# Weight sums moved out of the down projections, and another order of the last projection's products

## The reference, cut to what matters

```python
x = first_block(x, ...)     # pooled mixer, then conv_ffn: up 1024 -> 2 x 2816, conv, gelu gate, down
for i in range(2):          # second_block
    m = fox_mixer(h) if i == 0 else s5_mixer(h)      # 16-head attention with forget gates; state space
    x = x + rmsnorm(m)
    x = x + rmsnorm((silu(h @ w_gate) * (h @ w_up)) @ w_down)     # up2/dn2, then up3/dn3
```

## Time and profile before

| | us |
|---|---|
| runs | 1713.88, 1724.02, 1733.31 |
| median | 1724.02 |
| the profiled execution's own time | 1720.28 |
| its span, first to last instruction | 1718.2 |
| PE busy | 1629.2 (95%) |
| DVE busy | 1102.5 (64%) |
| ACT busy | 724.7 (42%) |
| POOL busy | 319.5 (19%) |

### The profile page before, as it was taken

One profiled execution on the slowest core, in us unless ns is written; L12 is line 12 of the kernel. 1 busy time (PEld: TensorE's weight loads), 2 busy tenths in 40 slices (PEclk: granted clock), 3 DMA queues, 4 the chain that ended last, 5 costly groups with the idle time before them and its releaser, 6 DMA issues.

```text
span 1718.2 us, 23609 instructions
## 1 busy us (share of the span) xinstructions
PE 1629.2 (95%) x9069; PEld 1379.5 (80%) x9069; DVE 1102.5 (64%) x1774; ACT 724.7 (42%) x1158; POOL 319.5 (19%) x833
## 2 busy tenths in 40 slices
PE   6499999998999999999999999996999999999997
PEld 5378888886877877778888888785888889999786
DVE  6988666665664677756333337564756687777776
ACT  4454433322344767744222222233224444444564
POOL 2011401001307777720111111111011000000000
PEclk8789999999999999999999999998999999999999
DMA  8922257877542222225678878889994235555664
GB/s 354 374 74 99 98 197 193 215 204 214 153 120 83 68 72 71 81 80 172 232 193 182 181 223 208 224 238 247 248 244 122 92 116 183 182 183 184 181 189 145
DMA packets 176961, 297.20 MB, mean 173 GB/s; under 512 B 31713, under 2 KB 115025, under 8 KB 173522
## 3 DMA queue, kind: packets, MB, share of 16 engines
q1 hardware_dynamic: 141842, 225.44, 39.8%
q0 software_dynamic: 20096, 62.92, 16.6%
q10 hardware_dynamic: 14912, 7.34, 1.7%
HBM read 277.84 MB, written 80.73 MB: 209 GB/s over the span
## 4 chain that ended last, share of the span: by engine, by line
PE 74%; DVE 11%; DMA 8%; ACT 3%; issue 2%; SPq 0%; POOL 0%; ACTq 0%; DVEq 0%
PE bank L2194 23%; PE bank L2196 22%; PE bank L2195 22%; DMA raw<-in_dn 3%; DMA u_scratch<-us 2%; DVE ada L1426 2%; DVE w_lo L1323 1%; PE bank L2557 1%; DMA cc<-in_s_c 1%; PE bank L2530 1%; DVE prod L1673 1%; DVE r_tab L1675 1%; DVE r_tab L1672 1%; ACT w_hi L853 1%; PE bank L2686 1%
## 5 line engine op out<-in xcount | busy, mean ns | idle before, releaser
L2194 PE MATMUL bank<-hh,w_hi 128*128 128x512 f32 (+1 forms) x1440 | 521.1, 362 | 7.3 <-DVE w_lo L1323 3.4
L2195 PE MATMUL bank<-hl,w_hi 128*128 128x512 f32 (+1 forms) x1440 | 517.4, 359 | 0.0
L2196 PE MATMUL bank<-hh,w_lo 128*128 128x512 f32 (+1 forms) x1440 | 517.0, 359 | 0.0
L1323 DVE TENSOR_TENSOR w_lo<-raw,w_hi 128x1024 fp32r<-128x1024 f32 x320 | 373.5, 1179 | 210.8 <-ACT w_hi L853 205.7
L853 ACT ACTIVATE w_hi<-raw 128x1024 fp32r<-128x1024 f32 x320 | 325.3, 1021 | 415.4 <-DMA raw<-in_dn 175.4
L2194 PEld LDWEIGHTS bank<-hh,w_hi 128*128 128x128 f32 x1440 | 274.2, 190 | 48.9 <-DVE w_lo L1323 3.8
L2196 PEld LDWEIGHTS bank<-hh,w_lo 128*128 128x128 f32 x1440 | 274.3, 190 | 39.9
L2195 PEld LDWEIGHTS bank<-hl,w_hi 128*128 128x128 f32 x1440 | 274.5, 191 | 39.0
L2194 PE MATMUL bank<-w_hi,hid 128*128 128x512 f32 x352 | 138.6, 394 | 0.9 <-ACT kt L1014 0.9
L2195 PE MATMUL bank<-w_lo,hid 128*128 128x512 f32 x352 | 137.1, 389 | 0.0
L2196 PE MATMUL bank<-w_hi,hid 128*128 128x512 f32 x352 | 137.1, 389 | 0.0
(11 more groups left out here) (352 smaller groups left out, 2570.6 us busy)
## 6 DMA issues: line engine op xcount, KB each, us to landing
raw<-in_up SPq DMA_DIRECT2D x94, 512.0 KB, 3.8
raw<-in_dn SPq DMA_DIRECT2D x55, 512.0 KB, 5.8
ada<-in_ada_w SPq DMA_DIRECT2D x24, 1024.0 KB, 8.3
v_v_scratch<-in_up POOLq DMA_DIRECT2D x30, 768.0 KB, 7.8
v_scratch<-in_dn POOLq DMA_DIRECT2D x24, 704.0 KB, 6.3
raw<-in_fox_in SPq DMA_DIRECT2D x32, 512.0 KB, 3.5
raw<-in_up SPq DMA_DIRECT2D x57, 256.0 KB, 2.9
raw<-in_s_w SPq DMA_DIRECT2D x24, 512.0 KB, 5.3
```

The source lines that it names most:

```text
L1323: dve.tensor_tensor(w_lo[:, n % RING, 0:w], raw[:, n % RING, 0:w], w_hi[:, n % RING, 0:w].bitcast(F32), ALU.subtract).then_inc(lo_done, 1)
L2194: pe.matmul(dst, w_h, r_h, start=first, stop=False, skip_group_check=True)
L2195: pe.matmul(dst, w_h, r_l, start=False, stop=False, skip_group_check=True)
L2196: return pe.matmul(dst, w_l, r_h, start=False, stop=last, skip_group_check=True)
```

## The change

It does two things. First, the order on POOL: the 56 up sums now come first and the 32 weight sums last. Of the up sums 24 wait for the slots 20 to 43 (counts 21 to 44, in up1), 8 for the value slots 68 to 75, and 24 lie between the turn tables: one after each table, a second one after each odd table. These last ones wait only for each other. The weight sums wait for the slots from 110 on (counts from 111, in up2). SP's two waits on `sum_step` are changed to fit. Second, the products of the last down projection run as P1 P5 P6 P7 P4 P3 P2, with the operands, banks, sources and the additions between them permuted; s4 is formed at place 1 and s3 at place 2.

```diff
-        A_RAW = [a11_s1[:, :, 0, :], s2[:, :, :], s3[:, :, :], a11_s1[:, :, 1, :], a12_a22[:, :, 1, :], s4[:, :, :],
+        A_RAW = [a11_s1[:, :, 0, :], a11_s1[:, :, 1, :], s2[:, :, :], s3[:, :, :], a12_a22[:, :, 1, :], s4[:, :, :],
...
-        PROD_BANK = (BX, BY, BW, BZ, BY, BZ, BX)
+        PROD_BANK = (BX, BZ, BY, BW, BY, BZ, BX)
...
-            sp.wait_ge(sum_step, 16 * (DOWN_SUMS + 8 * len(SUM_CHUNKS)))
+            sp.wait_ge(sum_step, 16 * UP_SUMS)
...
-            sources = (q3[0], v_dram[1], v_dram[2], v_dram[0], v_dram[3], q3[3], q3[2])
-            sp.wait_ge(sum_step, 16 * DOWN_SUMS)
+            sources = (q3[0], v_dram[0], v_dram[1], v_dram[2], v_dram[3], q3[3], q3[2])
+            sp.wait_ge(sum_step, 16 * (UP_SUMS + 32))
...
-                    if i in (2, 5):
-                        act.wait_ge(comb_done, 4 + c + 1)
+                    if i == 3:
+                        act.wait_ge(comb_done, 4 + len(A_CHUNKS) + c + 1)
...
                     if i == 1:
+                        own.add(dve.tensor_tensor(s4[:, k0:k1, :], a12_a22[:, k0:k1, 0, :], s2[:, k0:k1, :], ALU.add))
+                    if i == 2:
                         own.add(dve.scalar_tensor_tensor(s3[:, k0:k1, :], s2[:, k0:k1, :], -1.0, a12_a22[:, k0:k1, 1, :],
                                                          ALU.mult, ALU.subtract))
-                        own.add(dve.tensor_tensor(s4[:, k0:k1, :], a12_a22[:, k0:k1, 0, :], s2[:, k0:k1, :], ALU.add))
+                    if i in (1, 2):
...
-                        if s == 0 and i == 2:
+                    if s == 0 and i == 3:
+                        for j in range(2):
                             dve.wait_ge(p1_done, PAIRED + j + 1)
                             dve.tensor_tensor(u2[:, j, :], bank[BY[j]][:, :], p1[:, j, :], ALU.add).then_inc(y_step, 1)
-                        if s == 0 and i == 3:
+                    if s == 0 and i == 4:
+                        for j in range(2):
                             dve.wait_ge(y_step, Y_STEPS + j + 1)
                             dve.tensor_tensor(u3[:, j, :], bank[BW[j]][:, :], u2[:, j, :], ALU.add).then_inc(y_step, 1)
...
             for t, ((to, src, add), (j0, j1)) in enumerate(itertools.product(steps, SUM_CHUNKS)):
-                    pool.wait_ge(slot_mm, start + t + 1)
-                    pool.wait_ge(sum_step, 16 * (DOWN_SUMS + t))
+                    if t:
+                        pool.wait_ge(sum_step, 16 * t)
...
+                    yield
+
+            sums = up_sums()
+            for t in range(24):
+                pool.wait_ge(slot_mm, S_UP1 + 19 + t)
+                next(sums)
+            for t in range(KT):
+                pool.wait_ge(slot_mm, S_V + 1 + t)
+                next(sums)
             for k in range(PAIRS // 2):
                 turn_tables(k)
-            up_sums(S_UP2 + 2)
+                next(sums)
+                if k % 2:
+                    next(sums)
+            assert next(sums, None) is None
+            weight_sums(S_UP2 + 2)
...
-                    if i == 2:
+                    if i == 1:
                         pe.wait_ge(val_done, 2 * HT)
```

More of the change, by code:

```diff
@@ L85 @@
 Y_STEPS = 4 * PAIRED
-DOWN_SUMS = 32
 SUM_CHUNKS = ((2, 5), (5, 8), (8, 11), (12, 15), (15, 18), (18, 20), (20, 22))
+UP_SUMS = 8 * len(SUM_CHUNKS)
 PRODUCTS = 7
@@ L320, in build @@
         g_val, g_gate = scr[:, 2, :], scr[:, 3, :]
-        A_RAW = [a11_s1[:, :, 0, :], s2[:, :, :], s3[:, :, :], a11_s1[:, :, 1, :], a12_a22[:, :, 1, :], s4[:, :, :],
+        A_RAW = [a11_s1[:, :, 0, :], a11_s1[:, :, 1, :], s2[:, :, :], s3[:, :, :], a12_a22[:, :, 1, :], s4[:, :, :],
                  a12_a22[:, :, 0, :]]
-        A_LO = [a11_s1_lo[:, :, 0, :], s2_lo[:, :, :], s3_lo[:, :, :], a11_s1_lo[:, :, 1, :], a12_a22_lo[:, :, 1, :],
+        A_LO = [a11_s1_lo[:, :, 0, :], a11_s1_lo[:, :, 1, :], s2_lo[:, :, :], s3_lo[:, :, :], a12_a22_lo[:, :, 1, :],
                 s4_lo[:, :, :], a12_a22_lo[:, :, 0, :]]
@@ L1626, in down_products @@
                     i, s = divmod(idx, PER)
-                    if s == 0 and i >= 2:
+                    if s == 0 and i >= 3:
                         dve.wait_ge(slot_mm, first + idx)
-                    for j in range(2):
-                        if s == 0 and i == 2:
+                    if s == 0 and i == 3:
+                        for j in range(2):
                             dve.wait_ge(p1_done, PAIRED + j + 1)
                             dve.tensor_tensor(u2[:, j, :], bank[BY[j]][:, :], p1[:, j, :], ALU.add).then_inc(y_step, 1)
-                        if s == 0 and i == 3:
+                    if s == 0 and i == 4:
+                        for j in range(2):
                             dve.wait_ge(y_step, Y_STEPS + j + 1)
                             dve.tensor_tensor(u3[:, j, :], bank[BW[j]][:, :], u2[:, j, :], ALU.add).then_inc(y_step, 1)
-                        if s == 0 and i == 4:
+                        for j in range(2):
                             dve.wait_ge(y_step, Y_STEPS + 2 + j + 1)
                             dve.tensor_tensor(c22[:, j, :], bank[BZ[j]][:, :], u3[:, j, :], ALU.subtract).then_inc(y_step, 1)
+                    for j in range(2):
                         if s == 0 and i == 5:
@@ L2159, in weight_sums @@
                     pool.wait_ge(slot_mm, start + t + 1)
-                    if t:
-                        pool.wait_ge(sum_step, 16 * t)
+                    pool.wait_ge(sum_step, 16 * (UP_SUMS + t))
                     if add:
@@ L2166, in weight_sums, with up_sums @@
                         pool.dma_start(v_dram[to, m], src[m], max_dma_last_dim=4 * FH * P).then_inc(sum_step, 16)
-            def up_sums(start):
+            def up_sums():
                 gate, val = dram["up3"].rearrange("(j s) p c -> s j p c", s=2)
@@ L2181, in up_sums @@
                         pool.dma_start(dst, src).then_inc(sum_step, 16)
-            weight_sums(S_UP1 + 22)
+                    yield
[6 more added lines that the diff above has]
+                next(sums)
             for k in range(PAIRS // 2):
                 turn_tables(k)
-            up_sums(S_UP2 + 2)
+                next(sums)
[3 more added lines that the diff above has]
+            weight_sums(S_UP2 + 2)
             for i in range(KT):
```

## The result

The changed kernel takes 1770.07 us (median of 4 runs, 1764.16 to 1772.11) against 1720.65 for the kernel before (4 runs): a ratio of 1.0273, with a 95% interval of 1.0205 to 1.034. The profiled execution has a span of 1770.4 us against 1718.2, 52.2 more.

What follows compares the result with a forecast made beforehand. PE, busy 95% of the span, was taken to bound the kernel. 1720.3 + 69.3 (attention) + 2 (restart) - 15.5 (relief) = 1776 us, stated as 1778 between the profiled and median bases; range 1745 to 1820.

Steps and rivals of the forecast that it cites:

- The ring: Attention: SP's table stores, their landings, GpSimd's tables and sums set the pace; load 107 goes at 823, costing 69.3 us.
- the late start: Start of the attention: table 0 must follow sum 31, so it begins at 541 (535 to 545).
- the turns: Between turn tables: second sums after odd tables wait for the firsts, adding 51.1 us in all; turns average 17.9 us.
- Rival (c): Attention: the ring of weights absorbs longer turns, only the late start costs, 20 us; total 1725 us, chance 7%.
- rival (b): Attention: tables are quicker because VectorE starves, 11.5 us each in place of 13.5; total 1746 us, chance 12%.
- Rival (a): Attention: tables are slower beside a sum in flight, at most 50 us more; half gives 1803 us, chance 13%.
- The down projections: First and second down projections: relief of 2 us (0 to 6), most idle time being for ya, which no sum causes.
- S5: S5 mixer: without the sums' traffic it gains 12 us (5 to 20), 10 of idle time and 2 for the clock.
- The order of the products: Last down projection: the new order removes PE's wait for w_lo at its start, gaining 1.5 us (-1 to 2.3).
- The sum: Whole kernel: 69.3 us cost in the attention plus 2 for the restart, less 15.5 of relief elsewhere.
- the restart: After the attention's idle time: 2 us added for PE's lower granted clock.

Runs made afterwards that it cites:

- e1: The changed kernel, but GpSimd itself issues the store of each turn table, not SP's queue; 1691.03 us, ratio 0.9839 to the kernel before.
- e5: The kernel before with only the stores of the turn tables moved to GpSimd's queue, as a control; 1717.29 us, ratio 1.0004.
- e3: The changed kernel without the 8 sums beside the value slots ahead of table 0 (last 8 moved to up2); 1727.03 us, ratio 1.0047.
- e4: The changed kernel with one sum after each table, the 8 second ones moved to the start of up2; 1735.22 us, ratio 1.009.
- e2: The kernel before with only the new order of the last products; 1716.02 us, ratio 0.9984.
- e7: e1 with the weight sums starting 36 slots later, so they run through dn2 into S5; 1712.51 us, ratio 0.9961.
- e8: e6 with a pause: the last 5 up sums wait until slot 107 is done; 1686.65 us, ratio 0.9808 to the kernel before.
- e6: e1 with tables 0 to 7 computed beside dn1, and tables 8 to 15 carrying one sum inside and one behind; 1691.63 us, ratio 0.9825.

## Why the prediction was right, and where it was not

The forecast was 1778 us with 1745 to 1820; it is 1770.

**The ring: right.** I said that the attention would be paced by SP's stores, with load 107 going at 823: it goes at 829.4. e1 shows that it is this and not the traffic; e5 shows that before the ring had just kept up; e3 and e4 show that both terms, the late start and the turns, are there and add up. Rival (c) had the mechanism wrong and its price too low: the ring of weights absorbs neither, and the late start alone costs 43.2 us, not 20.

**The late start: the right size.** GpSimd begins table 0 at 539.39 (I said 541), its store goes at 549.37 (554), PE waits 24.5 us (20). Its timeline from sum 24 on:

```profile
486.65 1.51 POOL L2182 DMA_DIRECT2D v_v_scratch<-in_up  x1 [127.77 <-PE bank L2210]
495.88 1.22 POOL L2182 DMA_DIRECT2D v_v_scratch<-in_up  x1 [7.72 <-DMA v_v_scratch<-in_up]
509.91 1.14 POOL L2182 DMA_DIRECT2D v_v_scratch<-in_up  x1 [12.81 <-DMA v_v_scratch<-in_up]
...
528.05 0.73 POOL L2184 DMA_DIRECT2D v_v_scratch<-v_v_scratch  x1 [4.34 <-DMA v_v_scratch<-v_v_scratch]
533.05 0.73 POOL L2184 DMA_DIRECT2D v_v_scratch<-v_v_scratch  x1 [4.26 <-PE bank L2210]
538.67 0.73 POOL L2184 DMA_DIRECT2D v_v_scratch<-v_v_scratch  x1 [4.89 <-DMA v_v_scratch<-v_v_scratch]
539.39 0.12 POOL L2082 MEMSET turn_new<- 128x2 f32 x1
```

That it comes out so close is luck, for two errors of some 5 us cancel: the value slots came about 6 us earlier, since dn1 was shorter, and one add took 14.0 us (495.88 to 509.91) where I had put 8.0. The chain lasts 52.7 us instead of 48.4.

**The turns: 7 us too cheap.** From 539.4 to store 15 are 289.4 us; my terms gave 282. The eight turns after even tables last 15.3 us (13.3 to 17.1) where I had 15.9 less the 4 us spread over all, the seven after odd ones 22.5 (20.0 to 24.5) where I had 20.8. The step that was too small is the wait for the first sum of a pair: the seven lasted 55.4 us in all (four copies of 6.4 to 7.0, three adds of 9.1 to 10.0), where I had 44.8. The tables themselves were quicker than my sum had them, 206.6 us for all 16 (12.9 each), 5 less than 216 - 4; so rival (b) had the direction right and a third of the size. My 5.2 us for a copy is what a copy in the value stage takes (5.0 from 528.05 to 533.05), but in the attention even a smaller one, of 512 KB, took 6.4 as the first of a pair (564.51 to 570.95):

```profile
564.51 0.75 POOL L2184 DMA_DIRECT2D v_v_scratch<-v_v_scratch  x1 [0.56 <-POOL turn_new L2017]
570.95 0.70 POOL L2184 DMA_DIRECT2D v_v_scratch<-v_v_scratch  x1 [5.69 <-DMA v_v_scratch<-v_v_scratch]
```

SP had just issued the table's store and two loads back to back, and the copy went beside them. In e1, where the loads no longer come with the store, the same four copies take 4.1 to 5.2 us. That makes it likely that the loads are why, though e1 changes more than that; the adds, 8.1 to 10.7 us there, differ less. The Trainium skill, DMA: Bandwidth & Descriptors, section Anatomy of one DMA — SWDGE (gpsimd) path, gives as a fit 2.0 us plus the bytes at 436 GB/s, which makes an estimate of 3.8 us for 768 KB. The copies of this size in the changed kernel's value and attention stages took 5.0 to 7.0 us to the next issue, so here the fit is too low.

**Rival (a), tables slowed by a sum in flight: refuted.** Table 0 now starts 0.7 us after sum 31 was issued, as table 0 of before started beside the last weight sum, and takes 10 us (539.39 to 549.37) against 16.8 then. What differs is VectorE, which stands idle here for 44.5 us, until 555.78, and was busy there. With VectorE at work the answer is the same: in e1, where a sum goes out beside every table and VectorE is busy 140 of 200 us, the 16 tables take 13.7 us on average, and 13.8 in e5, where no sum is in flight. The rule of the Trainium skill on the shared SBUF interfaces (GPSIMD Engine Reference, Specifications) agrees with that.

**The down projections: the step that failed.** I gave them 2 us (0 to 6) with the argument that most of PE's idle time there is for ya, "which no sum causes". They gave 6.9 and 7.0 in the pair of profiles, and the wait for ya is smaller or gone (5.9 to 1.9 us, 4.2 to none). The chain of waits in dn1 shows how a sum could cause it, first of before:

```profile
392.36 9.13 DMA raw<-in_dn
401.68 0.85 issue
402.53 1.07 ACT w_new L1011 x2
...
404.53 0.96 ACT w_hi L853
...
406.66 1.16 DVE r_tab L1672
...
416.63 0.77 DVE q_tab L1675
417.63 1.05 issue
419.19 2.47 DVE ya L1344 x4
```

and of the changed kernel:

```profile
388.75 6.31 DMA raw<-in_dn
395.26 0.85 issue
396.11 1.06 ACT w_new L1011 x2
...
411.21 1.05 issue
412.26 0.28 DVE dd L1327
412.78 2.48 DVE ya L1344 x4
```

This is a ring of the same kind. A load waits in SP's queue behind the stores of S5 tables (lines 689 to 694), which wait for VectorE. VectorE's next tables stand behind the w_lo of that load. ya comes last in VectorE's stream, after those tables, and so carries every delay of the ring. A turn has one landing in it, 9.13 us before and 6.31 now. ya comes 6.4 us earlier: 2.8 by this landing, 3.6 because the load itself went earlier. The releaser named in the wait was VectorE, but behind it stands a DMA two steps back, and the sums were beside it.

That is a reading of two chains. How far it holds, all ten executions tell (PE's wait for ya in us; D in us):

| kernel | last sum issued | ya in dn1 | ya in dn2 | D |
|---|---|---|---|---|
| before | beyond D | 5.9 | 4.2 | 108.0 |
| e2 | beyond D | 1.8 | 2.8 | 105.6 |
| e5 | beyond D | none | 4.0 | 106.8 |
| e7 | beyond D | 0.4 | 2.2 | 105.5 |
| e1 | 46 us into D | 0.2 | 3.4 | 104.7 |
| e3 | 46 us into D | 0.7 | 3.1 | 105.1 |
| e4 | 47 us into D | 1.9 | 1.7 | 104.3 |
| e8 | as D starts | 0.3 | 1.6 | 103.0 |
| after | before D | 1.9 | none | 101.0 |
| e6 | before D | 1.2 | none | 101.1 |

For dn2 they bear it out. With sums all through, D is 106.5 us on average and ya is waited for each time; where the sums end before it, D is 101.0 and 101.1 and the wait is gone: 5.4 us. For dn1 they do not. The first three kernels all have the weight sums beside it until about 437, yet only before shows the wait of 5.9 us; e2 has 1.8 and e5 none. A is 162.6 to 169.6 us in these three (mean 165.6) and 159.1 to 164.3 in the seven with the early up sums (160.9). The means differ by 4.7, but the ranges overlap, and what makes the difference stays open. So my bound of 6 for both together was too low by about 4 us, and the rest of the 13.9 is the scatter of single executions, above all the long A of before.

**S5: right.** I said 12 us; the pair of profiles shows 13.0. The mean of E with sums in flight is 253.6 us (250.1, 257.0, 249.7, 257.7) and without them 234.2 (231.9 to 237.1), which makes 19, near my upper bound. **The order of the products: right**, 1.8 against 1.5, by the wait that I named.

**The sum.** I had +71.3 in the attention and -15.5 elsewhere, +55.8. It was +82.7 and -29.7, +53.0; the span grew by 52.2 (the remaining 0.8 lies outside the stages). Two terms were each some 11 to 14 us too small, with opposite signs, so that the total is this close is partly luck. Of the 11.4 us in the attention, 6.4 are load 107 (829.4 for 823) and 7.0 that load 76 went at 499.99 and no longer at 506.99; the 2 us for the restart show nowhere, as C is 271.0 us against 272.0. PE was also busy 20.5 us longer in B, most of it by the lower clock, for which I had nothing; since GpSimd's chain sets when load 107 goes, this took the place of idle time.

## What to carry to other kernels

Before work is put into an engine's idle time, ask which queue waits for that engine and what stands behind the waiting instruction: here the stretch had room on the DMA engines, and sums put before and between GpSimd's tables still cost 83 us, because a store that waited for GpSimd had the next weight loads behind it. Half of that came from the 8 sums that made the first table late (43.2 us in e4), half from those between the tables (38.9 us in e3), mostly from having to wait for the first of a pair. Moving that store to the queue of the engine that makes the data turned a loss of 2.7% into a gain of 1.6% (1.9% with the sums spread). Follow a wait back to the transfer in its ring before calling it independent of traffic, and take it from more than one execution: the wait of 5.9 us for ya in dn1 was in one of the three with the same sums beside it.

## What the runs showed of the hardware

After a wait of 24.5 us PE's granted clock was 0.50 in the stretch from 545 to 560 us, and in e6 a stretch of 20 us with a wait of 3.9 us had 0.83, against 1.00 in e8 without the wait. A single add of 768 KB in DRAM took 14.0 us to the next issue beside the four weight loads that SP issued between 494.88 and 499.99, where 8.45 was the mean of 14 adds of 768 and 512 KB before; and a load of 512 KB beside an add took 9.7 us, against a median of 3.4 for the loads of output weights in the kernel before. GpSimd's tables took no longer beside sums in flight (13.7 us, e1) than without (13.8, e5), but table 0, with a sum in flight each time, took 9.9 us in the changed kernel and in e4, where VectorE had nothing to do, and 12.0 in e1, where it had work.
